# Expert biases read once and spread on chip, second-bias product inside the expert loop, last expert's rows added by a product

## The reference, cut to what matters

```python
def sparse_moe(h, router_w, router_b, w1, b1, w2, b2):      # 512 tokens, 32 experts, TOP_K = 4
    logits = (hf @ router_w + router_b).astype(jnp.float32)
    top_val, top_idx = lax.top_k(logits, TOP_K)
    gate = jax.nn.softmax(top_val, axis=-1)
    ...                                                     # sort the 2048 (token, expert) pairs by expert
    def expert_block(args):
        e, toks, wts = args
        u = hf[toks] @ w1[e] + b1[e]                        # 1024 -> 2048
        g_, lin = u[:, :D_FF], u[:, D_FF:]
        g_ = jnp.minimum(g_, SWIGLU_LIMIT)
        lin = jnp.clip(lin, -SWIGLU_LIMIT, SWIGLU_LIMIT)
        y = ((lin + 1.0) * g_ * jax.nn.sigmoid(SWIGLU_ALPHA * g_)) @ w2[e] + b2[e]    # 1024 -> 1024
        return y * wts[:, None]
    ...                                                     # sum the rows of each token
x = x + g2 * sparse_moe(h, ...)                             # g2: one factor for each of the 1024 columns
```

## Time and profile before

| | us |
|---|---|
| median of 3 runs (2125.32 to 2132.86) | 2125.63 |
| profiled execution, time | 2124.19 |
| its span, first to last instruction | 2122.5 |
| TensorE busy (share of the span) | 1951.7 (92%) |
| VectorE busy | 639.0 (30%) |
| ScalarE busy | 365.9 (17%) |
| GpSimd busy | 195.5 (9%) |

### The profile page before, as it was taken

How to read it: one execution, slowest core, us unless ns; L and a number is a source line. 1 busy time by engine, 2 the same in 40 slices (tenths; PEclk the granted TensorE clock), 3 DMA queues, 4 the chain that set the end, 5 groups by cost and what they waited for, 6 DMA issues and landing times.

```text
span 2122.5 us, 37796 instructions
## 1 busy us (share of the span) xinstructions
PE 1951.7 (92%) x15926; PEld 1045.7 (49%) x15926; DVE 639.0 (30%) x1668; ACT 365.9 (17%) x823; POOL 195.5 (9%) x240
## 2 busy tenths in 40 slices
PE   5999999998999999999998888889898888989989
PEld 4576655753444444444343433434343343765854
DVE  6346757322120202122121111202020115257240
ACT  2115631432110101011000000101000011142110
POOL 1020000000002121211111111110101010000000
PEclk8979999999899999999999999999999989999999
DMA  9711222321579999999999999999999984200001
GB/s 301 225 47 60 80 80 80 159 75 64 204 258 385 384 390 374 385 380 361 383 370 377 377 372 376 371 374 369 376 369 370 339 263 130 80 1 1 1 0 40
DMA packets 155314, 510.96 MB, mean 241 GB/s; under 512 B 22098, under 2 KB 99272, under 8 KB 105992
## 3 DMA queue, kind: packets, MB, share of 16 engines
q1 hardware_dynamic: 132112, 472.94, 60.2%
q0 software_dynamic: 17088, 26.48, 5.8%
q10 hardware_dynamic: 5944, 9.09, 1.2%
HBM read 489.47 MB, written 18.48 MB: 239 GB/s over the span
## 4 chain that ended last, share of the span: by engine, by line
PE 63%; SPq 15%; DMA 14%; DVE 4%; issue 2%; ACT 1%; POOL 0%; ACTq 0%; DVEq 0%; POOLq 0%
PE bank L1417 14%; DMA ring<-in_exp_w_dram 13%; PE bank L390 10%; PE bank L1433 8%; PE bank L398 7%; SPq L888 7%; PE bank L793 5%; SPq L892 4%; PE bank L552 3%; SPq L883 3%; PE bank L574 2%; PE bank L563 2%; PE bank L764 1%; PE bank L374 1%; DVE arena L740 1%
## 5 line engine op out<-in xcount | busy, mean ns | idle before, releaser
L1417 PE MATMUL bank<-ring,arena 128*32 128x512 f32 x5696 | 643.0, 600 | 72.3 <-DMA ring<-in_exp_w_dram 69.0
L1417 PEld LDWEIGHTS bank<-ring,arena 128*32 128x32 f32 x5696 | 180.0, 111 | 511.7 <-issue 359.2
L1433 PE MATMUL bank<-ring,arena 128*32 128x256 f32 x5696 | 325.3, 386 | 24.5 <-DMA ring<-in_exp_w_dram 15.9
L1789 DVE COPY arena<-bank 128x12 f32<-128x12 f32 (+2 forms) x32 | 5.4, 170 | 911.9 <-PE bank L1381 880.1
L1433 PEld LDWEIGHTS bank<-ring,arena 128*32 128x32 f32 x5696 | 217.3, 111 | 122.8 <-DMA ring<-in_exp_w_dram 22.1
L390 PE MATMUL bank<-hT,ring 128*128 128x512 f32 x448 | 210.3, 622 | 13.2 <-DVE hT L770 7.5
L1036 POOL DMA_INDIRECT expert_sums<-arena,dst_r x89 | 137.9, 1550 | 380.3 <-ACT arena L1172 355.2
L398 PE MATMUL bank<-ring,hT 128*128 128x256 f32 (+1 forms) x768 | 156.4, 363 | 0.0
L390 PEld LDWEIGHTS bank<-hT,ring 128*128 128x128 f32 x448 | 87.7, 199 | 119.3 <-issue 115.8
L1154 ACT ACTIVATE arena<-bank 128x384 f32<-128x384 f32 (+2 forms) x64 | 26.5, 464 | 693.2 <-PE bank L1398 693.2
L398 PEld LDWEIGHTS bank<-ring,hT 128*128 128x128 f32 x768 | 135.6, 190 | 18.4 <-issue 2.4
(11 more groups left out here) (325 smaller groups left out, 1551.9 us busy)
## 6 DMA issues: line engine op xcount, KB each, us to landing
ring<-in_exp_w_dram SPq DMA_DIRECT2D x384, 1024.0 KB, 26.0
ring<-in_ada_w_dram SPq DMA_DIRECT2D x24, 1024.0 KB, 10.9
ring<-in_w_in_dram SPq DMA_DIRECT2D x23, 1024.0 KB, 9.9
ring<-in_w_out_dram SPq DMA_DIRECT2D x8, 1024.0 KB, 4.9
arena<-in_exp_b_dram SPq DMA_DIRECT2D x128, 64.0 KB
expert_sums<-arena POOLq DMA_DIRECT2D x5, 512.0 KB, 4.7
arena<-in_x_dram ACTq DMA_DIRECT2D x1, 2048.0 KB, 12.5
ring<-in_w_in_dram SPq DMA_DIRECT2D x8, 256.0 KB, 5.0
```

The lines of the kernel that those rows point to most:

```text
L1417: mm = pe.matmul(bank[g][QUAD * c:QUAD * (c + 1), :].rearrange("p (h n) -> p h n", h=2), rowsT[:, k, QUAD * g:QUAD * (g + 1)], w[:, :, SW ...
L1433: mm = pe.matmul(bank[4 + g // 2][QUAD * c:QUAD * (c + 1), SW * (g % 2):SW * (g % 2 + 1)], actT[:, j, g, QUAD * q:QUAD * (q + 1)], w[:, c, :],
```

## The change

Three parts.

First biases: one set of four loads before the loop puts b1 of all experts on chip, expert e on partition e of each of the four groups of 32 partitions. VectorE turns it once in blocks of 32x32 (`b1T`). In each iteration VectorE reads the expert's number into a register, copies that expert's 16 columns (`b1_one`) and turns a broadcast of them back, which gives the same tile as before, 128x512, in `b1_rows`. SP's queue has no bias loads in the loop.

Second biases: the product `b2_keep` x `gatesT` moves into iterations 10 to 17, one block of 128 columns in each, into bank 7; VectorE adds it, times g2, into `resT`.

Last place: its scaled rows are not added into `expert_sums`. ScalarE writes them to `y_last`, VectorE makes `hot_last`, which is one where a row's token is the column's, and TensorE multiplies the two into the eight banks (32 products with 32 contracted rows, each on one of four row groups); VectorE adds them, times g2, into `resT`. The wait for the adds of GpSimd is for place 30's at the latest. The tiles of `expert_sums` are then turned by plain transposes.

The diff, cut to its core (left out are new semaphores, `B2_AT = range(10, 18)`, and the same changes for the extra loop):

```diff
@@ -164,8 +164,11 @@
         route = room(4608, [NT, NEXP, 4])
-        b1_all = [room(5120 + 512 * n, [512]) for n in range(2)]
...
+        b1T, b1_rows, b1_one = room(5120, [16, NEXP]), room(5632, [512]), room(7808, [16])
         u_in = room(OM + 1024, [4, 512])
+        y_last, hot_last = u_in[:, 0, :].rearrange("p (g n) -> p g n", g=2), u_in[:, 2:4, :]
         posmT = room(OM + 1024, [S], NEXP)
@@ -878,12 +886,6 @@
-            def bias_in(e, n, signal):
-                for c in range(4):
-                    sp.dma_start(b1_all[n][QUAD * c:QUAD * (c + 1), :].rearrange("p (e h n) -> p e h n", e=1, h=2),
-                                 b1_cols[c, bass.ds(e, 1), :, :].unsqueeze(0).to_broadcast([QUAD, 1, 2, SW]))\
-                      .then_inc(signal, 16)
...
             def first_rows(e, k, signal):
@@ -909,13 +911,12 @@
             sp.wait_ge(o_acc, O_MOBA)
-            bias_in(0, 0, b1_in[0])
+            for c in range(4):
+                sp.dma_start(b1_rows[QUAD * c:QUAD * (c + 1), :].rearrange("p (h n) -> p h n", h=2), b1_cols[c])\
+                  .then_inc(b1_in, 16)
             sp.wait_ge(order_ok, 1)
...
                 e = sp.value_load(order_i[0:1, n:n + 1], min_val=0, max_val=NEXP - 1)
-                if n >= 2:
-                    sp.wait_ge(main.u_in, n - 1)
-                bias_in(e, n % 2, b1_in[n % 2])
                 for k in range(8):
...
@@ -1048,7 +1048,7 @@
                     fetch(main, n + 3, QUADS[n + 2])
-                if n >= 1:
+                if 1 <= n < NEXP:
                     put(main, n, PARTS_BY[n - 1], dst_r[(n - 1) % 4], QUADS[n - 1])
@@ -1181,10 +1181,16 @@
                 if n >= 1:
-                    if n >= 2:
-                        act.wait_ge(main.free, n - 1)
-                    rows_done(main, n, meta_r[(n - 1) % 4], QUADS[n - 1])
-            act.wait_ge(main.free, NEXP)
+                    if n < NEXP:
+                        if n >= 2:
+                            act.wait_ge(main.free, n - 1)
+                        rows_done(main, n, meta_r[(n - 1) % 4], QUADS[n - 1])
+            act.wait_ge(main.dst, NEXP)
+            act.wait_ge(main.y, NEXP)
+            for g in range(QUADS[-1]):
+                act.activation(y_last[:, g, :], bank[4 + g // 2][:, SW * (g % 2):SW * (g % 2 + 1)], ACT.Copy,
+                               scale=meta_r[(NEXP - 1) % 4][:, g, 2:3]).then_inc(y_last_ok, 1)
+            act.wait_ge(main.free, NEXP - 1)
             act.wait_ge(r_dv, 1)
@@ -1481,6 +1487,11 @@
                     pe.wait_ge(main.y_ok, PARTS_BY[n - 1])
+                if n in B2_AT:
+                    t = n - B2_AT[0]
+                    pe.wait_ge(main.at_ok, 2 * n)
+                    pe.matmul(bank[7][:, :], b2_keep[:, P * t:P * (t + 1)], gatesT, start=True, stop=True)\
+                      .then_inc(b2_t, 1)
                 if n + 1 < NEXP:
@@ -1491,6 +1502,8 @@
                         pe.wait_ge(main.at_ok, 2 * n)
+                    if n in B2_AT:
+                        pe.wait_ge(b2_ok, n - B2_AT[0] + 1)
                     turn_rows(main, 16 * (n + 2), QUADS[n + 1])
@@ -1499,7 +1512,19 @@
                     second_layer(main, QUADS[n - 1], wait_slot, True)
-            pe.wait_ge(main.y_ok, PARTS_BY[NEXP])
...
+            pe.wait_ge(main.u_in, NEXP)
+            pe.wait_ge(main.at_ok, 2 * NEXP)
+            pe.wait_ge(hot_last_ok, 1)
+            pe.wait_ge(y_last_ok, QUADS[-1])
+            for j in range(2):
+                for g in range(QUADS[-1]):
+                    for c in range(4):
+                        rows = slice(QUAD * c, QUAD * (c + 1))
+                        mm = pe.matmul(bank[2 * c + j][:, :], y_last[rows, g, P * j:P * (j + 1)], hot_last[rows, g, :],
+                                       start=(g == 0), stop=(g == QUADS[-1] - 1))
+                mm.then_inc(last_t, 1)
+            pe.wait_ge(last_ok, ND)
             pe.wait_ge(r_dv, 1)
@@ -1518,14 +1543,10 @@
-            pe.wait_ge(gT_ok, 1)
-            for t in range(ND):
-                pe.matmul(bank[t][:, :], b2_keep[:, P * t:P * (t + 1)], gatesT, start=True, stop=False)
             for i in range(NT):
...
                 for t in range(ND):
-                    mm = pe.matmul(bank[t][:, i * P:(i + 1) * P], y_rows[i][:, P * t:P * (t + 1)], ident[:, :],
-                                   start=False, stop=(i == NT - 1))
+                    mm = pe.transpose(bank[t][:, i * P:(i + 1) * P], y_rows[i][:, P * t:P * (t + 1)], ident[:, :])
                 mm.then_inc(y_used, 1)
@@ -1792,9 +1813,15 @@
-            def swiglu(sg, n, bias, quads):
+            def biases(sg, e):
...
+                settle(sg, dve.tensor_copy(b1_one.unsqueeze(2), b1T[:, :, bass.ds(e, 1)]))
+                settle(sg, dve.transpose(b1_rows.rearrange("p (k q) -> p k q", q=QUAD),
+                                         bc(b1_one.unsqueeze(2), [P, 16, QUAD])))
...
+            def swiglu(sg, n, quads):
                 for g in range(quads):
-                    ins = dve.tensor_tensor(u_in[:, g, :], bank[g][:, :], bias, ALU.add)
+                    ins = dve.tensor_tensor(u_in[:, g, :], bank[g][:, :], b1_rows, ALU.add)
                 ins.then_inc(sg.u_in, 1)
@@ -1843,7 +1870,19 @@
             who_at(2)
+            dve.wait_ge(b1_in, 64)
+            link(dve.transpose(b1T.rearrange("p k e -> p (k e)"), b1_rows))
             for n in range(NEXP):
+                if n in B2_AT:
+                    t = n - B2_AT[0]
+                    dve.wait_ge(b2_t, t + 1)
+                    dve.scalar_tensor_tensor(out=resT[:, t, :], in0=bank[7][:, :], scalar=mod[:, 40 + t:41 + t],
+                                             in1=resT[:, t, :], op0=ALU.mult, op1=ALU.add).then_inc(b2_ok, 1)
+                if n == 0:
+                    e = 0
+                else:
+                    e = dve.value_load(order_i[0:1, n:n + 1], min_val=0, max_val=NEXP - 1)
+                biases(main, e)
                 if n + 2 < NEXP:
@@ -1852,10 +1891,22 @@
                     who_at(n + 3)
-                dve.wait_ge(b1_in[n % 2], 64 * (n // 2 + 1))
                 dve.wait_ge(w1_used, 8 * (n + 1))
-                swiglu(main, n + 1, b1_all[n % 2], QUADS[n])
-            dve.wait_ge(main.free, NEXP)
+                swiglu(main, n + 1, QUADS[n])
+            to_last = meta_r[(NEXP - 1) % 4]
+            for g in range(QUADS[-1]):
+                for i in range(NT):
+                    ins = dve.tensor_scalar(hot_last[:, g, P * i:P * (i + 1)], iota_c[:, :], float(P * i), to_last[:, g, 1:2],
+                                            ALU.add, ALU.is_equal)
+            ins.then_inc(hot_last_ok, 1)
+            dve.wait_ge(b2_ok, ND)
+            for j in range(2):
+                dve.wait_ge(last_t, j + 1)
+                for t in range(j, ND, 2):
+                    dve.scalar_tensor_tensor(out=resT[:, t, :], in0=bank[t][:, :], scalar=mod[:, 40 + t:41 + t],
+                                             in1=resT[:, t, :], op0=ALU.mult, op1=ALU.add).then_inc(last_ok, 1)
+            dve.wait_ge(last_ok, ND)
+            dve.wait_ge(main.free, NEXP - 1)
             extra = dve.value_load(extra_i[0:1, 0:1], min_val=0, max_val=31)
```

More of the change, by code:

```diff
@@ L825, in dve_out @@
                 ins.then_inc(res_ok, 1)
+        B2_AT = range(10, 10 + ND)
+        assert QUADS[-1] == 2
         OUT_PARTS = ((0, 4), (4, 6), (6, 8))
@@ L1890, in _ @@
                     at = dve.value_load(pos_i[0:1, 0:1], min_val=0, max_val=NEXP - 1)
+                    of = dve.value_load(exp_i[0:1, 0:1], min_val=0, max_val=NEXP - 1)
+                    biases(over, of)
                     dve.tensor_copy(route_o[:, :, :], route[:, :, bass.ds(at, 1), :].rearrange("p i e c -> p i (e c)"))
```

11 lines of the change are left out of this document (6 added, 5 removed).

## The result

The changed kernel takes 2059.2 us (median of four runs, 2055.4 to 2060.95) against 2125.48 for the kernel before: a ratio of 0.9678, 95% interval 0.9652 to 0.9704. The profiled execution took 2055.4 us. Its trace has 58.1 of the 68.8 us between the two profiled executions in the loop, and 10.6 between the last second layer and the first add of the row tiles.

The account below looks back on a forecast made before the run. TensorE was taken to bound the loop's early places, transfers the later ones from about 912 us. Gains of 58 (loop) and 8 (tail) make 66, from 2124.19 to 2058, as a median 2060 us; range 2040 to 2098.

Parts of the forecast that it names:

- The loop, 58 us: Places up to 30: without bias loads, place 30's second layer starts at 1633 instead of 1691.03, gaining 58 us.
- The account: Loop after 912 us: landing time plus 20.7 places at the transfers' 34.4 us each gives place 30's second layer at 1629.
- the queue at 912 us: Transfers at 912 us: some 18 us of built-up waiting vanishes, so a weight load lands after 4.8 us.
- the price of the biases: Bias loads in the loop: removing them saves the transfers 2.0 us a place, 36.4 to 34.4; bounds 0.8 and 3.7.
- the second path: Loop through TensorE: place 18 starts at 1184.8, then 153 loads bring place 30's second layer to 1631.
- unevenness: End of the loop: a little irregularity moves place 30's second layer from 1630 to 1633.
- The product at places 10 to 17: Second-bias product before the second layer: gap of 4.5 to 4.9 us instead of 2.4, TensorE at 34.4 us a place.
- The slower case: Places 10 to 17: VectorE's chain before the second layer costs 14 us more a place, giving 2148 us; chance 0.05.
- The tail, 8 us: Behind the last second layer: one-hot product and plain transposes end at 1732 against 1740.3, gaining 8 us.
- The first rival: Loop: bias loads cost only their lone 0.8 us a place, so a place takes 35.6 us; 2092 us, chance 0.22.
- The clock rival: Tail: transposes don't engage the fast clock, so the eight norm products after them cost 6 us more; 2066 us, chance 0.05.
- the signs named: Trace checks, including landings near 5 us until 1190, a 5 us gap at places 10 to 17, 19 to 21 to transposes.

Follow-up runs that it names:

- biases_only: The kernel before with only the first-bias part: biases loaded once and spread by VectorE, second-bias product behind the loop, last place scattering; 2066.5 us, ratio 0.9714.
- the last kernel: The changed kernel with TensorE's register read and branch before its wait for the last adds, and VectorE's biases before its wait for the second-bias product; 2053.4 us.
- product_only: The kernel before with only the second-bias product moved into the loop and plain transposes behind it; bias loads and last scatters stay; 2115.3 us, ratio 0.9948.
- own_rows_one: The kernel before with one 0.262 MB load a place, from own rows of the first weights, in place of four bias loads; 2080.4 us.

## Why the prediction was right, and which of its terms were not

**The loop, 58 us: right in mechanism; the total was hit by luck, since two errors mostly cancel.** Place 30's second layer was to start at 1633 and did at 1632.94. The account said 912 + 4.8 + 20.7 x 34.4 = 1629. With what was measured it is 912.3 + 15.1 + 20.7 x p, so p = 34.1. Wrong was the queue at 912 us: I took it as gone because nine places had saved a set each, which would have needed the transfers to be behind during all of those. They were not behind enough. The median landing of the loads issued from 700 to 731, before and then after:
```profile
ring<-in_exp_w_dram SPq DMA_DIRECT2D x8, 1024.0 KB, 10.5
```
```profile
ring<-in_exp_w_dram SPq DMA_DIRECT2D x10, 1024.0 KB, 9.1
```
In the kernel before the landings stay between 10.5 and 11.8 us from 640 to 840, and between 9.0 and 10.0 with the change; only from there to 912 do they rise, to 22.8 and 15.1. The queue was built later, and it shrank by 7.7 us instead of 18: 10.3 us too much gain. Wrong the other way was **the price of the biases**: 2.0 us, against 2.7 to 3.0 by the period, or 2.4 by the account's own mean over the loop ((1691.03 - 912 - 22.8) / 20.7 = 36.5, less 34.1). With it a place came to 34.4 us instead of 34.1, 6 us too little gain over 20.7 places. The 4 us left between the two, 1629 and 1633, are what the prediction had added for the second path and for unevenness, with no row behind the latter. The readings I had gave 0.8, 2.1 to 2.7 and 3.7; the stretches of the full queue came nearest, and I took a value under them.

**The product at places 10 to 17: about right, for another reason.** Predicted a gap of 4.5 to 4.9 us; it was 3.70. The failed link is the register load, 0.8 us in the chain which hides beside the multiply-add. Still TensorE took 33.94 us a place there ((1183.88 - 912.33) / 8), against 34.4 predicted, because of a term that the prediction did not have: the clock. In biases_only these places take 31.5 ((1172.03 - 912.45) / 8, less 1.0 that its first layers lose to transfers at places 15 and 16). Of the 2.5 us above that, 1.4 are the longer gap and 1.1 the second layers. The eight of them took 90.0 us in the changed kernel, seven slowed by the clock, and 81.0 in biases_only, two slowed. One of the latter's at the full clock:
```profile
965.08 10.57 PE L1425 MATMUL bank<-ring,arena 128*32 128x256 f32 x192 [0.30 <-DVE dst_r L1785]
```
Place 18 started at 1183.88; predicted 1184.8.

**The slower case** could not decide here: what TensorE lost was hidden. biases_only and the last kernel reached place 18 at 1172 and 1180, and their second layer of place 30 starts within 1 us of the changed kernel's.

**The tail, 8 us: 10.6 measured, and credited too widely.** The one-hot product took 3.71 us (forecast 5, between 3.5 and 7), TensorE's register and branch behind the adds 4.7 (4.4), the 32 transposes 5.01 in one execution and 6.60 in another (6 to 7); in that other execution the stretch is 20.3 us, 9.1 below the kernel before. But I gave the whole to the second and third part together. In product_only the stretch is 17.8 us already, no longer than in the changed kernel. The third part trades the last scatters and the late row tiles for eight adds and an exposed register read and branch.

**The first rival** (the biases at their lone price) asked for more than 35.5 us a place without biases; it was 34.0. That price was right as engine time and wrong as a measure of what the queue loses: the set took 7.2% of the engines over 11 us, the single load of own_rows_one 7.7% over the same stretch, and in the full queue the set costs 2.7 to 3.0 and the single load 0.8 to 1.1 us. **The clock rival** fell too: behind a stage of transposes alone, at a mean granted clock of 0.71 in one execution and 0.53 in another, the norm's products ran at 1.00. The clock even rose while only transposes ran: in the changed kernel it stands at 0.50 up to 1669 us and at 1.00 from 1670 to 1671. Windows of the changed kernel, then the transposes in its other execution:
```profile
1666.00:1672.00 6.00, 5.46 (x34) 5.23 (x34) 0.24 (x1) 0.00 (x0) 0.00 (x0) 0.71 0.68 212
1674.00:1680.00 6.00, 6.00 (x14) 1.88 (x14) 4.51 (x13) 3.78 (x6) 0.88 (x1) 1.00 1.10 350
```
```profile
1667.00:1674.00 7.00, 6.89 (x34) 6.81 (x34) 0.00 (x0) 0.00 (x0) 0.00 (x0) 0.53 0.78 246
```

Of the signs named, three did not show. The landings up to 1190 were 15 us and not near 5, and the gap was 3.7 us and not 5. The 19 to 21 us to the transposes do not fit the prediction's own sum, which has the transposes start 14.1 us behind the last second layer and end at 21; measured were 13.8 and 18.8. The others did show.

## What to carry to other kernels

When one queue paces a loop, price a small load by the period of the loop with and without it, or by stretches of the full queue, never by its lone engine time: here a 64 KB load cost 0.55 to 0.7 us beyond its bytes, a 1 MB load nothing that 2 MB loads would save. Ask also from when on the queue is behind: only savings after that moment shorten it. And work put on an engine that waits for that queue is free up to the wait, as three kernels with different stalls and one loop's end show. A tail's wait, in contrast, is replaced by the next one in line, so build the variant without the last refinement too.

## What the runs showed of the hardware that I had not expected

- Small loads: 0.55 to 0.70 us each beyond their bytes in a full queue at 64 KB, a load of 256 KB 0.8 to 1.1 us with its bytes, no difference between 1 MB and 2 MB (34.16 us a place against 33.93 to 34.28). About half of the cost goes when they are issued from another queue. What in the queue makes it stays open; packet size and repeated reads are excluded as the main cause.
- A register load behind a multiply-add of 0.75 us in VectorE's program cost nothing. A register load (0.49 us) and a branch (3.74 us) on TensorE, behind a wait with no work beside them, cost 4.7 us; once they stood ahead of the wait, 1.0 us of it was left in one kernel and 2.2 us in another.
- The granted clock falls although TensorE is hardly idle. Behind gaps of 3.3 to 3.7 us filled with small products, at most 0.7 us of them idle, seven of eight second layers were slowed, in each of three kernels (the changed one, product_only and the last one); behind gaps of 2.3 us it was two of eight, in the kernel before and in biases_only. A slowed one of 192 instructions took 11.7 to 13.3 us instead of 10.57. Whether the gap's length or the added product does it, no run separates.
- Four row groups of 32 rows do overlap: 32 instructions of 32x512 in 3.71 us at a granted clock of 1.00, 0.12 us each, where 16 of the same shape, one row group only, had taken 14.02 at 0.50, 0.88 each (at the full clock an estimated 0.44, half of that).
